# One decoder layer on one core: tokens first in the load queue, in four buffers; projection weights behind the conditioning slices; conditioning rows copied by two engines

## What is computed

```python
mod = silu(c) @ w_ada + b_ada                 # 9 conditioning rows, 6 x 1024 columns
sh1, sc1, g1, sh2, sc2, g2 = split(mod, 6)
h = rms_norm(x, norm1_g) * (1 + sc1) + sh1
z = h @ w_in                                  # q, k, v, o, gates, the two conv halves
u = ga * sigmoid(gb)                          # the conv half: 31 taps, layer norm, swish
hc = swish(layer_norm(causal_conv(u)))
hm = layer_norm(mlstm(q, k, v, ig, fg)) * sigmoid(o)
x = x + g1 * (concat(hm, hc) @ w_out)
x = x + g2 * moe(rms_norm(x, norm2_g) * (1 + sc2) + sh2)
y = rms_norm(x, final_g)                      # moe: top 1 of 4 groups, top 2 of its 8 experts
```

## Time and profile before

| | |
|---|---|
| median of 3 runs | 1129.07 us (1126.12 to 1129.82) |
| the profiled execution | 1126.61 us, of which the span shown in the profile is 1124.9 |
| mean granted TensorE clock of the span | 0.924 of full speed |
| TensorE busy | 980.4 us, 87% of the span |
| VectorE, ScalarE busy | 749.5 us, 509.7 us |
| moved by DMA | 215.37 MB |

### The profile page before, as it was taken

The page is one execution under the profiler, slowest core; times in us unless marked ns, Lnnn a source line. Parts: engine busy times, 40 slices in busy tenths (PEclk is TensorE's granted clock), DMA queues, the critical chain, the costliest instruction groups (busy, mean ns, idle before and its releaser), DMA issues.

```text
span 1124.9 us, 13181 instructions
## 1 busy us (share of the span) xinstructions
PE 980.4 (87%) x5089; PEld 785.8 (70%) x5089; DVE 749.5 (67%) x1011; ACT 509.7 (45%) x700; POOL 240.2 (21%) x261
## 2 busy tenths in 40 slices
PE   5599999999999679998998815699999989999764
PEld 2398979799999466665555414588888778888521
DVE  3530039988898542555554348699999799999647
ACT  4542141212111550432222103488888688888524
POOL 0000000000000000000000001366666846666320
PEclk9699999999999777999999956799999999999878
DMA  7943511121110620111113195399999989997585
GB/s 295 392 180 152 222 38 38 38 38 38 38 38 22 210 76 1 57 57 58 65 56 121 53 230 218 141 372 380 376 396 378 370 325 379 399 377 280 215 332 207
DMA packets 65491, 215.37 MB, mean 191 GB/s; under 512 B 14304, under 2 KB 35440, under 8 KB 47230
## 3 DMA queue, kind: packets, MB, share of 16 engines
q1 hardware_dynamic: 54622, 197.52, 47.3%
q0 software_dynamic: 10800, 16.93, 4.1%
HBM read 202.81 MB, written 34.49 MB: 211 GB/s over the span
## 4 chain that ended last, share of the span: by engine, by line
PE 72%; DVE 9%; DMA 7%; ACT 5%; issue 5%; POOL 2%; SPq 0%; POOLq 0%; DVEq 0%; ACTq 0%
PE ps L1951 25%; PE ps L1460 15%; PE ps L857 10%; PE ps L1479 7%; PE ps L1447 3%; DMA xt<-in_x_prompt 2%; DMA expert_results<-ysb,scur 1%; PE ps L1918 1%; PE ps L783 1%; DVE elo L1243 1%; PE ps L760 1%; DMA out<-caug 1%; PE ps L931 1%; DMA draw<-in_w_down 1%; PE ps L800 1%
## 5 line engine op out<-in xcount | busy, mean ns | idle before, releaser
L1243 DVE TENSOR_TENSOR elo<-eraw,ehi 128x1024 fp32r<-128x1024 f32 x148 | 174.1, 1219 | 0.0
L1860 DVE SCALAR_TENSOR_TENSOR z<-z,wdT 128x1024 f32<-128x1024 f32 x120 | 144.7, 1276 | 0.0
L1152 ACT ACTIVATE ehi<-eraw 128x1024 fp32r<-128x1024 f32 x148 | 144.5, 1068 | 0.0
L1951 PE MATMUL ps<-hhi,whi 128*128 128x344 f32 x576 | 124.2, 324 | 6.2 <-ACT hhi L1721 3.2
L1951 PE MATMUL ps<-hhi,wlo 128*128 128x344 f32 x576 | 123.5, 323 | 0.0
L1951 PE MATMUL ps<-hlo,whi 128*128 128x344 f32 x576 | 122.7, 322 | 0.1
L1702 ACT ACTIVATE z<-ps 128x1032 f32<-128x1032 f32 x24 | 24.8, 1035 | 214.1 <-PE ps L1951 204.8
L1079 POOL IOTA ioti<- 128x128 int32 x1 | 0.2, 239 | 497.6 <-DVE marks L1229 497.6
L1951 PEld LDWEIGHTS ps<-hhi,whi 128*128 128x128 f32 x576 | 97.7, 190 | 9.0 <-issue 6.0
L1951 PEld LDWEIGHTS ps<-hhi,wlo 128*128 128x128 f32 x576 | 98.8, 191 | 0.0
L1951 PEld LDWEIGHTS ps<-hlo,whi 128*128 128x128 f32 x576 | 96.7, 189 | 0.5 <-DVE hlo L1831 0.5
(11 more groups left out here) (383 smaller groups left out, 1697.5 us busy)
## 6 DMA issues: line engine op xcount, KB each, us to landing
eraw<-in_w_gate SPq DMA_DIRECT2D x37, 1024.0 KB, 7.5
eraw<-in_w_up SPq DMA_DIRECT2D x37, 1024.0 KB, 13.7
draw<-in_w_down SPq DMA_DIRECT2D x36, 1024.0 KB, 14.5
wada<-in_w_ada SPq DMA_DIRECT2D x24, 1024.0 KB, 9.6
wraw<-in_w_in SPq DMA_DIRECT2D x12, 1024.0 KB, 5.5
y<-expert_results SPq DMA_DIRECT2D x8, 1024.0 KB, 8.3
xt<-in_x_prompt SPq DMA_DIRECT2D x8, 512.0 KB, 5.4
wout<-in_w_out SPq DMA_DIRECT2D x1, 4096.0 KB, 15.8
```

The lines of the kernel that those rows point to most:

```text
L1152: act.activation(ehi[:, b, :, k, :], eraw[:, wb(e), :, k, :], ACT.Copy).then_inc(sem("ehi_ready"), 1)
L1243: dve.tensor_tensor(elo[:, wb(e), :, k, :], eraw[:, wb(e), :, k, :], ehi[:, b, :, k, :].bitcast(F32), ALU.subtract)\
L1860: dve.scalar_tensor_tensor(out=z[:, GB0 + b, PAD:SC], in0=z[:, U0 + b, w:w + T], scalar=wdT[:, b, w:w + 1], in1=z[:, GB0 + b, PAD:SC], op0 ...
L1951: mm = pe.matmul(ps[0:n, bank + c, 0:TW], w(k), h[:, k, c * TW:(c + 1) * TW], start=first, stop=last)
```

## The change

`xt` has four buffers, and the wait of a token load on `xn_done` reaches four tiles back. The loads of the small vectors (`vector_loads`) are issued behind token 3 and slice 2, not first; their transposes and copies stand behind token 5. Slice k's products follow the transposes of tile k + 1, not of tile k. Each of the first two blocks of projection weights is issued when slice 6 or slice 7 has landed; the gate weights and `m0` follow the second pair of blocks. In `mod_rows(0)` ScalarE copies the first two row groups and VectorE the other two. `mod_rows(0)` stands ahead of `hi(0)`, and `w_lo(0)` behind the first scaled block.

```diff
-        xt = sb(stA, "xt", [P, 2, D])
+        xt = sb(stA, "xt", [P, 4, D])
...
+            def vector_loads():
+                for at, n, v in (...):
+                    load(vecs[at:at + n, :], ..., "vec_in")
+                load(wdw[:, :], w_dw, "vec_in")
+                load(bi[:, :], ...); load(bf[:, :], ...)
...
             for t in range(NT):
-                if t >= 2:
-                    sp.wait_ge(sem("xn_done"), t - 1)
-                load(xt[0:rows[t], t % 2, :], x_d[t], f"x_in{t % 2}")
+                if t >= 4:
+                    sp.wait_ge(sem("xn_done"), t - 3)
+                load(xt[0:rows[t], t % 4, :], x_d[t], f"x_in{t % 4}")
                 if t:
                     ada_load(t - 1)
-            load(wraw[:, 0, :, :], w_in_v[:, :, C0_CONV:C0_CONV + 256], "wraw_in0")
-            load(wraw[:, 1, :, :], w_in_v[:, :, C0_CONV + 256:C0_CONV + 512], "wraw_in1")
-            load(wgt[:, :, :], ..., "wgt_in")
-            load(m0t[:, :], ..., "m0_in")
+                if t == 3:
+                    vector_loads()
+            for u in range(2):
+                sp.wait_ge(sem(f"wada_in{6 + u}"), 16)
+                load(wraw[:, u, :, :], w_in_v[:, :, C0_CONV + 256 * u:C0_CONV + 256 * (u + 1)], f"wraw_in{u}")
...
             for u in range(2):
                 w_in_load(1, u)
+            load(wgt[:, :, :], ..., "wgt_in")
+            load(m0t[:, :], ..., "m0_in")
...
ScalarE, mod_rows(g):
-                for j in range(4):
+                for j in range(4 if g else 2):
                     act.activation(modr[32 * j:32 * j + 9, :], ps[32 * j:32 * j + 9, ACC[g], :], ACT.Copy)
...
+            mod_rows(0)
             hi(0)
-            mod_rows(0)
...
VectorE, ahead of modulation(0):
-            w_lo(0)
+            dve.wait_ge(sem("ada_used"), KD)
+            dve.wait_ge(step("modr_zero"), after("modr_zero"))
+            for j in range(2, 4):
+                dve.tensor_copy(modr[32 * j:32 * j + 9, :], ps[32 * j:32 * j + 9, ACC[0], :])
...
                 if k:
                     h_lo(k - 1)
+                else:
+                    w_lo(0)
...
TensorE, token loop:
-                if t < KD:
-                    ada(0, t)
+                if t:
+                    ada(0, t - 1)
+                if t == 5:
+                    (transposes of vecs and wdw)
```

More of the change, by code:

```diff
@@ L198, in build @@
         wdw = sb(stA, "wdw", [CW, CB * P])
-        xt = sb(stA, "xt", [P, 2, D])
+        xt = sb(stA, "xt", [P, 4, D])
         xn = sb(stA, "xn", [P, 2, D])
-        taken = D + P + CB * P + 4 * D
+        taken = D + P + CB * P + 6 * D
         sb(stA, "blocks_0_7", [P, 8 * ZW - taken])
@@ L1540, in _ @@
             load(c9[1:9, :], c_sample, "c_in")
[L1541 to L1547, removed]
+            def vector_loads():
+                for at, n, v in ((0, MB, b_ada), (MB, KD, norm1_g), (MB + KD, KD, norm2_g), (MB + 2 * KD, H, mh_g),
+                                 (MB + 2 * KD + 4, CB, b_dw), (MB + 2 * KD + 8, CB, cln_g),
+                                 (MB + 2 * KD + 12, CB, cln_b)):
+                    load(vecs[at:at + n, :], v if len(v.shape) == 2 else v.rearrange("(b p) -> b p", p=P), "vec_in")
+                load(wdw[:, :], w_dw, "vec_in")
+                load(bi[:, :], b_ig.rearrange("(h o) -> h o", o=1), "gbias_in")
+                load(bf[:, :], b_fg.rearrange("(h o) -> h o", o=1), "gbias_in")
             def ada_load(n):
@@ L1556, in _ @@
             for t in range(NT):
-                if t >= 2:
-                    sp.wait_ge(sem("xn_done"), t - 1)
-                load(xt[0:rows[t], t % 2, :], x_d[t], f"x_in{t % 2}")
+                if t >= 4:
+                    sp.wait_ge(sem("xn_done"), t - 3)
+                load(xt[0:rows[t], t % 4, :], x_d[t], f"x_in{t % 4}")
                 if t:
                     ada_load(t - 1)
-            load(wraw[:, 0, :, :], w_in_v[:, :, C0_CONV:C0_CONV + 256], "wraw_in0")
-            load(wraw[:, 1, :, :], w_in_v[:, :, C0_CONV + 256:C0_CONV + 512], "wraw_in1")
-            load(wgt[:, :, :], w_in_v[:, :, 4 * H * DH:4 * H * DH + 2 * H], "wgt_in")
-            load(m0t[:, :], m0.rearrange("b h -> h b"), "m0_in")
+                if t == 3:
[3 more added lines that the diff above has]
+                load(wraw[:, u, :, :], w_in_v[:, :, C0_CONV + 256 * u:C0_CONV + 256 * (u + 1)], f"wraw_in{u}")
             def w_in_load(m, u):
@@ L1576, in _ @@
                 w_in_load(1, u)
+            load(wgt[:, :, :], w_in_v[:, :, 4 * H * DH:4 * H * DH + 2 * H], "wgt_in")
+            load(m0t[:, :], m0.rearrange("b h -> h b"), "m0_in")
             for n in range(2 * KD, 3 * KD):
@@ L1672, in _ @@
                 b, n = t % 2, rows[t]
-                act.wait_ge(sem(f"x_in{b}"), 16 * (t // 2 + 1))
+                act.wait_ge(sem(f"x_in{t % 4}"), 16 * (t // 4 + 1))
                 if t >= 2:
                     act.wait_ge(sem("xT_done"), t - 1)
-                chain(act.activation(xn[0:n, b, :], xt[0:n, b, :], ACT.Square, accum_out=ssq[0:n, b, 0:1]))
+                chain(act.activation(xn[0:n, b, :], xt[0:n, t % 4, :], ACT.Square, accum_out=ssq[0:n, b, 0:1]))
                 chain(act.activation(ssq[0:n, b, 1:2], ssq[0:n, b, 0:1], ACT.Ln, bias=epst[0:n, :], scale=1.0 / D))
@@ L1775, in _ @@
                .then_inc(step("c9T_ready"), 1)
-            dve.wait_ge(step("vT_ps"), after("vT_ps"))
-            chain.last(dve.tensor_copy(vT[:, :], ps[:, 5, 0:NV]))
-            chain(dve.tensor_copy(wdT[:, :, :], ps[:, 5, P:P + 32 * CB].rearrange("p (b w) -> p b w", b=CB)[:, :, 0:CW]))
             def xnorm(t):
@@ L1782, in xnorm @@
                 dve.wait_ge(sem("rstd_ready"), t + 1)
-                dve.tensor_scalar(xn[0:n, b, :], xt[0:n, b, :], ssq[0:n, b, 1:2], None, ALU.mult)\
+                dve.tensor_scalar(xn[0:n, b, :], xt[0:n, t % 4, :], ssq[0:n, b, 1:2], None, ALU.mult)\
                    .then_inc(sem("xn_done"), 1)
@@ L1800, in _ @@
                    .then_inc(sem("xT_copied"), 1)
+                if t == 5:
+                    dve.wait_ge(step("vT_ps"), after("vT_ps"))
+                    chain.last(dve.tensor_copy(vT[:, :], ps[:, 5, 0:NV]))
+                    chain.last(dve.tensor_copy(wdT[:, :, :],
+                                               ps[:, 5, P:P + 32 * CB].rearrange("p (b w) -> p b w", b=CB)[:, :, 0:CW]))
             def modulation(g):
@@ L1819, in _ @@
             chain.wait()
-            w_lo(0)
+            dve.wait_ge(sem("ada_used"), KD)
+            dve.wait_ge(step("modr_zero"), after("modr_zero"))
+            for j in range(2, 4):
+                dve.tensor_copy(modr[32 * j:32 * j + 9, :], ps[32 * j:32 * j + 9, ACC[0], :]).then_inc(sem("modr_ready"), 1)
             modulation(0)
@@ L1904, in _ @@
             mm.then_inc(step("c9T_ps"), 1)
[L1905 to L1909, removed]
             pe.wait_ge(step("c9T_ready"), after("c9T_ready"))
@@ L1936, in _ @@
                 mm.then_inc(sem("xT_done"), 1)
-                if t < KD:
-                    ada(0, t)
+                if t:
+                    ada(0, t - 1)
+                if t == 5:
+                    pe.wait_ge(sem("vec_in"), 16 * 8)
+                    pe.transpose(ps[:, 5, 0:NV], vecs[:, :], ident[0:NV, 0:NV])
+                    for b in range(CB):
+                        mm = pe.transpose(ps[:, 5, P + 32 * b:P + 32 * b + CW], wdw[:, b * P:(b + 1) * P],
+                                          ident[0:CW, 0:CW])
+                    mm.then_inc(step("vT_ps"), 1)
             ada_transpose(0)
```

## The result

The changed kernel takes 1121.04 us in the median of five runs (1117.12 to 1121.69), the kernel before 1129.07 (1126.12 to 1129.82): ratio 0.9933, 95% interval 0.9918 to 0.9948, so 7.5 us less by the ratio, where the prediction worked out 7.6. Its profiled execution took 1121.69 us, span 1119.9.

What follows compares the result with a forecast made beforehand. Before 66 us the load queue was taken to bound the kernel, afterwards TensorE; 4.6 us (TensorE's end) plus 3.0 (last product to first projection) made 7.6 us less, giving 1120.0 us, chosen between 1119.0 and 1121.5, range 1115.5 to 1126.0.

Steps and rivals of the forecast that it cites:

- The queue: Loads before 66 us: earlier token start and closed hole at 12 to 14 us bring slice 6 4.7 us earlier.
- the vectors that move behind this (about 0.10 MB, 0.25 us): Small vector loads, moved behind the first tokens into the load stream, cost 0.25 us of the queue's gain.
- TensorE's end: Last conditioning product, at the end of the load-bound stretch: ends at 38.4 us against 42.99, 4.6 us earlier.
- the two cases: Last conditioning products take 1.04 or 1.90 us by granted clock, so the end comes at 38.0 or 38.8 us.
- From the last product on: Last conditioning product to end of first scaled block: 4.55 us instead of 7.58, 3.0 us less.
- The cover of 2.2 us for the projection weights: Before projection 0: whi is ready by 40.7 us and needed at 42.95, 2.2 us of cover.
- falls of the clock that move with the start: Later stretches: granted-clock falls may move with the start; 3.70 us of spread allowed, half to each side.
- the prediction's own signs: Before the long run: last product at 38 to 39 us, first hlo at 43.5 to 44.5, run from about 58.5.
- its smaller gain: Stretch before projection 0: lower TensorE clock throughout, or copies not side by side; gain 5 to 7 us, chance 0.22.
- The slow queue: Rival, load queue: a deep queue runs slower, slice 6 lands 5.2 us later; gain 2 to 3.5 us, chance 0.10.
- The copies that hold each other up: Rival in mod_rows(0): two engines' copies of one PSUM bank don't run side by side, 1.2 us less; within smaller gain's 0.22.
- the late projection weights: Rival before projection 0: second weight block lands late, projection 0 starts 7.7 us later, 1135 us; chance 0.05.

Runs made afterwards that it cites:

- the taps split: Changed kernel with the conv taps (31 rows of 2 KB) loaded as 16 and 15 rows instead of in one load: 1117.87 us, ratio 0.9913.
- no waits on the slices: Changed kernel without SP's waits on slices 6 and 7 ahead of the projection weights: unbroken TensorE run starts at 59.19 us instead of 59.71.
- the rows on one engine: Changed kernel with all four row copies of group 0 on ScalarE again: unbroken TensorE run starts at 60.70 us, 0.99 us later.

## Why the prediction came out

*The queue.* "4.7 us" for slice 6 measured 38.23 to 35.14, 3.1. The start and the closed hole were right: the rate has no gap, and with the taps split slice 6 lands at 33.11, 0.4 ahead of what was worked out. The mis-sized term is "the vectors that move behind this (about 0.10 MB, 0.25 us)". It spread the bytes over 16 engines; 63 KB of them go by one, and the shown price is 2.0 us at slice 6 and 1.9 at the last product. A sign of it stood in the profile of before: TensorE waited 3.1 us for that small load, up to 8.36.

*TensorE's end.* Forecast 4.6, measured 3.48: slice 6's lateness (1.6), less the 0.4 that the higher clock of the last products gave back (1.04 us, the better of the two cases).

*From the last product on.* Forecast 3.0, measured 2.88. The copies took 1.42 us side by side (1.4 from the line between two other copies), `w_lo(0)`, costed at 0.1 to 0.2, cost nothing that shows: the first `hlo` starts 1.13 us behind the end of the first scaled block, 1.12 before. The cover of 2.2 us for the projection weights was 2.3.

*To the end.* From 59.71 to 214.58 every piece is as long as before. Then 1.53 us go in a block of 360 matmuls. The block in the chain before, then in that of the changed kernel:

```profile
220.96 57.10 PE ps L1951 x360
```

```profile
214.58 58.63 PE ps L1965 x360
```

What follows the block again takes as long (846.8 and 846.7 us). TensorE pauses for 2.6 us ahead of the block in both kernels; afterwards the granted clock stayed at 1.00 in one and fell in the other, to 0.66 in the mean of 215 to 220 us, that is, 1.2 GHz for two thirds of it (before, then after):

```profile
220.00:225.00 5.00, 4.04 (x25) 4.04 (x26) 4.64 (x4) 4.90 (x6) 0.00 (x0) 1.00 0.00 0
```

```profile
215.00:220.00 5.00, 5.00 (x24) 5.00 (x23) 3.38 (x3) 4.93 (x5) 0.00 (x0) 0.66 0.00 0
```

The block took 57.1 us in all four profiles with the old queue, where it starts at 219 to 223 us. Of the nine with a changed queue, where it starts at 212 to 218, seven have 58.6, and two 57.1 (the taps split, and no waits on the slices). So the loss may come with the change, by the moment at which the block starts; what decides it is open. The prediction had allowed for falls of the clock that move with the start, in later stretches.

So the sum that came out at 7.6 was 6.35 in the profile at 59.71 us and 4.9 at its end. The medians are 8.0 apart, since the profiled execution of the changed kernel is the slowest of its five, and that of the kernel before lies below its median. That 1121.04 came so near to 1120.0 is in part chance. Of the prediction's own signs, several were missed by about 1 us: the last product ended at 39.51 (38 to 39 expected), the first `hlo` started at 45.34 (43.5 to 44.5), the run at 59.71 (58.5), and not every later stretch was as long as before. The 6.35 lies in the band of its smaller gain, for a reason that this band didn't name.

*The rivals.* The slow queue is out: 428 and 407 GB/s with loads queued throughout. The copies that hold each other up are out by the rows on one engine and by the copies themselves, two in 1.20 us and two in 1.42, begun 0.06 us apart; the late projection weights by the 2.3 us of cover. The prediction's slower case was never near.

## What to carry to other kernels

When small loads are moved into a full queue, look at how each is spread over the DMA engines, not at its bytes: one that goes by a single engine cost 0.2 us or less ahead of the stream here, and 2.0 in the middle of it. Parts of a change can lean on one another: the copies on two engines brought 0.73 us more with the sample token's work moved ahead of the last products than without; cost them as a chain, not as a list. With a gain below 1% the start of a long unbroken run in the profile tells edits apart that the times can't. But compare the landing of the loads and the granted clock first, since a single profile can be off in either: slice 6 was 3.7 us late once, and the turn differed by 0.46 us by its clock alone.

## What the runs showed of the hardware

In the middle of a full queue a load of 31 rows, 63 KB, puts the landing of a 1 MB load about 6 MB behind it back by 2.0 us (35.14 against 33.11), and a second one by 3.7 more (38.80); as 16 and 15 rows it delays nothing that shows. Ahead of the stream the one load costs 0.2 us or less, whether the queue has a hole behind it (38.23 against 38.03) or not (36.66 against 36.49).

ScalarE and VectorE copied rows of one PSUM bank, in different groups of 32 partitions, side by side: two 9x512 copies each, in 1.20 and 1.42 us, where four on ScalarE alone took 2.43.
